# Pacing indirect stores, larger pieces for the down weights, and a later start of the loads of result rows, in a two-layer decoder kernel

## The reference, cut to what matters

```python
def moe_swiglu(hn, w_router, w_gate, w_up, w_down):      # 8 experts, top 2, hidden width 3584
    xt = hn.reshape(T, D)                                # T = 256, D = 1024
    top_logit, top_idx = lax.top_k((xt @ w_router).astype(jnp.float32), TOP_K)
    gates = jax.nn.softmax(top_logit, axis=-1)
    ...                                                  # rows sorted by expert, padded to blocks
    def expert_block(args):
        xb, e = args
        hid = jax.nn.silu(xb @ w_gate[e]) * (xb @ w_up[e])
        return hid @ w_down[e]
    ...                                                  # y[token] += gate * row, for both choices
```

## Time and profile before

| | us |
|---|---|
| median of 3 runs | 1377.39 (1375.36 to 1378.34) |
| the profiled execution, its own time | 1371.37 |
| its span, first to last instruction | 1369.5 |
| TensorE busy | 1314.4 (96%) |
| VectorE, ScalarE, GpSimd busy | 360.5, 243.4, 53.7 |

### The profile page before, as it was taken

How to read it: one execution, slowest core, us unless ns; L and a number is a source line. 1 busy time by engine, 2 the same in 40 slices (tenths; PEclk the granted TensorE clock), 3 DMA queues, 4 the chain that set the end, 5 groups by cost and what they waited for, 6 DMA issues and landing times.

```text
span 1369.5 us, 32426 instructions
## 1 busy us (share of the span) xinstructions
PE 1314.4 (96%) x14601; PEld 860.1 (63%) x14601; DVE 360.5 (26%) x505; ACT 243.4 (18%) x364; POOL 53.7 (4%) x47
## 2 busy tenths in 40 slices
PE   6998999999899689999999999999999999999998
PEld 6997899988777335855755764774572353354244
DVE  5875555554874501101101101100100110110111
ACT  5463544443642000000000000000000000000000
POOL 0001000000000130000000000000000000001500
PEclk9999999999999899999999999999999999999999
DMA  9972465564521789699999999999999999999996
GB/s 322 350 262 59 148 191 186 185 229 161 201 76 62 305 314 346 255 418 368 407 418 417 406 416 418 404 412 420 407 411 420 398 409 420 405 407 418 407 409 255
DMA packets 128647, 442.52 MB, mean 323 GB/s; under 512 B 9396, under 2 KB 55812, under 8 KB 112132
## 3 DMA queue, kind: packets, MB, share of 16 engines
q1 hardware_dynamic: 122352, 424.75, 80.2%
q10 hardware_dynamic: 4820, 11.53, 2.3%
q0 software_dynamic: 1344, 4.20, 0.8%
HBM read 434.12 MB, written 12.08 MB: 326 GB/s over the span
## 4 chain that ended last, share of the span: by engine, by line
PE 79%; DMA 9%; DVE 4%; ACT 3%; issue 3%; SPq 1%; ACTq 0%; POOL 0%; DVEq 0%; POOLq 0%
PE bank L1701 38%; PE bank L1713 16%; PE bank L1344 7%; PE bank L1345 6%; PE bank L1346 6%; DMA dn<-in_moe_w_down 4%; DMA raw<-in_moe_w_gate 3%; ACT w_hi L569 2%; DMA raw<-in_moe_w_up 2%; PE bank L1601 1%; PE bank L1549 1%; SPq L443 1%; DVE w_lo L836 1%; PE bank L1482 1%; PE bank L1691 0%
## 5 line engine op out<-in xcount | busy, mean ns | idle before, releaser
L1701 PE MATMUL bank<-raw,xT 128*32 128x512 f32 (+1 forms) x4608 | 452.9, 539 | 8.9 <-issue 4.6
L1701 PEld LDWEIGHTS bank<-raw,xT 128*32 128x32 f32 x4608 | 194.4, 110 | 255.5 <-issue 206.0
L1713 PE MATMUL bank<-dn,hidT 128*32 128x256 f32 x5376 | 294.5, 379 | 2.3 <-DMA dn<-in_moe_w_down 2.2
L1713 PEld LDWEIGHTS bank<-dn,hidT 128*32 128x32 f32 x5376 | 215.9, 110 | 80.0 <-DMA dn<-in_moe_w_down 7.6
L1315 DVE TENSOR_TENSOR e_hid<-e_silu,bank 128x512 f32<-128x512 f32 (+1 forms) x48 | 26.9, 616 | 556.6 <-PE bank L1701 556.6
L836 DVE TENSOR_TENSOR w_lo<-raw,w_hi 128x2048 fp32r<-128x2048 f32 x62 | 141.5, 2291 | 107.5 <-ACT w_hi L569 107.4
L1701 PE MATMUL bank<-up_more,xT 128*32 128x384 f32 (+1 forms) x1536 | 157.2, 539 | 1.0 <-DMA up_more<-in_moe_w_gate 1.0
L1344 PE MATMUL bank<-ht_hi,w_hi 128*128 128x256 f32 x480 | 134.2, 280 | 4.7 <-DVE w_lo L909 3.2
L1345 PE MATMUL bank<-ht_lo,w_hi 128*128 128x256 f32 x480 | 133.4, 278 | 0.0
L1346 PE MATMUL bank<-ht_hi,w_lo 128*128 128x256 f32 x480 | 133.4, 278 | 0.0
L569 ACT ACTIVATE w_hi<-raw 128x2048 fp32r<-128x2048 f32 x62 | 118.6, 1918 | 46.2 <-PE bank L1346 42.4
(11 more groups left out here) (262 smaller groups left out, 835.8 us busy)
## 6 DMA issues: line engine op xcount, KB each, us to landing
dn<-in_moe_w_down SPq DMA_DIRECT2D x112, 1024.0 KB, 15.0
raw<-in_moe_w_gate SPq DMA_DIRECT2D x48, 1024.0 KB, 20.5
raw<-in_moe_w_up SPq DMA_DIRECT2D x48, 1024.0 KB, 15.8
raw<-in_moe_w_gate SPq DMA_DIRECT2D x48, 768.0 KB, 12.5
raw<-in_moe_w_up SPq DMA_DIRECT2D x48, 768.0 KB, 10.5
up_more<-in_moe_w_gate SPq DMA_DIRECT2D x16, 1024.0 KB
up_more<-in_moe_w_up SPq DMA_DIRECT2D x16, 1024.0 KB
raw<-in_hgrn_w_in SPq DMA_DIRECT2D x15, 1024.0 KB, 12.8
```

Of the source, the lines that this page charges most:

```text
L1701: ins = nc.tensor.matmul(out_banks[j][GTOK * c:GTOK * c + GTOK, 0:w], xT[:, j, kt, :], chunk[:, c], start=kt == 0, stop=kt == KT - 1)
L1713: ins = nc.tensor.matmul(banks[6 + j // 2][GTOK * c:GTOK * c + GTOK, 256 * (j % 2):256 * (j % 2) + 256], hidT[sup][:, g, m, :], dn[:, i % ...
```

## The change

Three edits. (1) Each of GpSimd's 16 indirect stores of token rows is issued only after one more up chunk of item 0 has been used. (2) A down chunk puts rows 2p and 2p + 1 of its 256 into partition p, which are 8 KB in one piece. To have the hidden units in the matching order, the array's column group c takes hidden columns 64c to 64c+63 of every 256, and VectorE's transposes into `hidT` pick the even and the odd ones apart; they are now one for each of the three row groups, so `hidT_ready` counts 6 in an item instead of 2. (3) GpSimd's wait for the stored items is followed by a wait for the last item's last transposes, before the four indirect loads of result rows.

```diff
     def down_source(e, i):
         r = 256 * i
-        return a["moe_w_down"][0][bass.ds(e, 1), r:r + 256, :].rearrange("e (k p) c -> p (e k) c", p=P)
+        return a["moe_w_down"][0][bass.ds(e, 1), r:r + 256, :].rearrange("e (p k) c -> p (e k) c", k=2)
...
                     for c in range(4):
+                        pool.wait_ge(up_used, 8 * t + 4 * i + c + 1)
+                        pool.sem_inc(pool_pace, 1)
                         to = bass.IndirectOffsetOnAxis(ap=slot[:, t, i, c:c + 1], axis=0)
...
             pool.wait_ge(y_stored, n_before * 16)
+            pool.sem_inc(pool_pace, 1)
+            pool.wait_ge(hidT_ready, n_before * (2 * GRPS) + 2 * GRPS)
             pool.sem_inc(pool_pace, 1)
...
-                    nc.vector.transpose(hidT[sup][:, :, :, :].rearrange("p j m t -> p j (m t)"), e_hid[:, :, 0:w]).then_inc(hidT_ready, 1)
-                    dve.wait_ge(hidT_ready, n * 2 + (sup + 1))
+                    for j in range(GRPS):
+                        nc.vector.transpose(hidT[sup][:, j, :, :].rearrange("p (m k) t -> p m k t", k=2),
+                                            e_hid[:, j, 0:w].rearrange("p (m i k) -> p m k i", k=2, i=GTOK)).then_inc(hidT_ready, 1)
+                    dve.wait_ge(hidT_ready, n * (2 * GRPS) + (GRPS * sup + GRPS))
...
-                chunk = up_slot(i)[:, 0:4 * w].rearrange("p (m c i) -> p c m i", c=4, i=GTOK)
+                chunk = up_slot(i)[:, 0:4 * w].rearrange("p (m c i) -> p c m i", c=4, i=2 * GTOK)
...
                     if i == 0:
                         pe.wait_ge(yb_ready, n * 2 + 1)
-                        pe.wait_ge(hidT_ready, n * 2 + 1)
+                        pe.wait_ge(hidT_ready, n * (2 * GRPS) + GRPS)
                     if i == 8:
-                        pe.wait_ge(hidT_ready, n * 2 + 2)
+                        pe.wait_ge(hidT_ready, n * (2 * GRPS) + 2 * GRPS)
```

## The result

The changed kernel takes 1357.95 us (median of 4 runs, 1355.14 to 1359.29), the kernel before beside it 1377.87. The ratio is 0.9854, with a 95% interval of 0.9832 to 0.9877. Forecast were 1360.0 us, within 1354 to 1372.5. The profiled execution has a span of 1353.2 us, against 1369.5, and a time of 1357.36 us.

What follows compares the result with a forecast made beforehand. The prediction took TensorE's pace of 108.4 us an item as the floor, with DMA engines nearly as full. 11.0 + 6.4 + 0 = 17.4 us off 1371.37 gave 1354.0, plus 6.0 carried over: 1360.0 us, range 1354 to 1372.5.

Steps and rivals of the forecast that it cites:

- The paced stores, -11.0: Item 0's up products: spacing the 16 stores removes the slow stretch of TensorE, 11.0 us off.
- each store slows TensorE: Item 0's up products: a store slows TensorE by itself, so pacing only spreads the 11.0 us, gain 0.
- the pile does: Item 0's up products: the pile of unfinished stores slows TensorE, so pacing gains all 11.0 us.
- 8 KB pieces, -6.4: Down chunks' transfers: 0.061 us less for each of 105 chunks, 6.4 us off.
- The loads of result rows, 0: Last item: four stops of some 3.7 us go, but the same bytes delay down chunks instead; gain 0.
- The covers: Last down products: GpSimd's later chain stays hidden with 3.6 us of slack; the three transposes' extra time is hidden too, cost 0.
- B: Rival, item 0: the slow stretch stays, belonging to the first pass through the loop; only 6.4 comes, 1371.0 us; chance 0.17.
- C: Rival, down chunks: the size of a piece is worth nothing, 11.0 alone comes, 1366.4 us; chance 0.12.
- E: Rival: slow stretch stays and piece size is worth nothing, no change, 1377.4 us; chance 0.07.
- D: Rival, the tail: loads of result rows land late and the last additions wait, slower, 1387 us; chance 0.06.

Runs made afterwards that it cites:

- the serial one: Changed kernel with each of the 16 stores issued when the one before it has landed, without regard to TensorE: 1359.76 us.
- late burst: Changed kernel with all 16 stores in one burst after 9 up chunks of item 0: 1357.47 us, and 1368.47 us when run again in a later session.
- the kernel with early loads: Changed kernel with the loads of result rows begun when the last item but one is stored, as before: 1355.69 us.
- the 4 KB run: Changed kernel with down chunks in 4 KB pieces, the old order of hidden rows and the old transposes: 1365.13 us.
- the loads in two pairs: Changed kernel with the second pair of result-row loads issued after GpSimd's first addition: 1358.39 us.
- two bursts of 8: Changed kernel with the 16 stores in two bursts, at up chunks 1 and 9 of item 0: 1357.85 us, and 1364.98 us when run again.

## Why the prediction was right, point by point

The sum was 17.4 us off the profiled execution's span; the items' time is 17.6 shorter. The median moved by more, 19.9 us, and why isn't known. That it fell only 2.1 us from the forecast is in part luck: the prediction put the median 6.0 us above the profiled execution's time, and here it stands 0.6 above, while that execution itself took 1357.36 us instead of 1354.0.

- *The paced stores, -11.0.* Measured -11.1 by item 0's up products in the two profiles, -10.9 and -11.4 by undoing and doing the edit alone. The choice between "each store slows TensorE" and "the pile does" was made by the first stores of the burst running beside full pace, and its outcome held: paced, the stores cost nothing. That it is the pile of unfinished stores isn't shown. The only run that held the pile at one store, the serial one, fell in the session in which a burst did no harm; there the late burst's stores landed after 6.0 us (the median) and were issued every 1.27, so that by an estimate four or five were unfinished at once, and nothing slowed. Two of the readings were also coarser than told: the 102 matmuls "at full pace" took 12.26 us where 10.9 is full pace (0.1073 each), so that the slowing starts before the first gap; and "the DMA engines are not full" is true of 490 to 495 us only, for their share is 1.00 from 480 to 484 and 0.82 from 484 to 490. Full engines alone don't do it all the same, as TensorE keeps its pace beside them for all of items 1 to 3. That the 11 us would reach the end also held: in the changed kernel the DMA engines still run dry before the first down products (0 GB/s from 540 to 545 us). But the gain isn't to be had in every session: in one of five, going by the time of the kernel before, a burst cost nothing.
- *8 KB pieces, -6.4.* Measured -6.7 with the edit undone (by the medians of the same session 9.4, against the kernel with early loads, with more noise); the rates are 418 to 419 against 408 to 410 GB/s, as read from the old trace. It was the reading of two kinds of transfer in one trace, side by side, that gave the number before the change was run. The rule of the Trainium skill in DMA: Bandwidth & Descriptors, Specifications, that transfers are at line rate from 512 bytes on, doesn't agree with these rows: 4 KB pieces moved 2.4% slower than 8 KB pieces of the same tensor. The measurement decides, with the reserve that the rows' order changed along with the size; in a stream that is the bound for 800 us, 2.4% of a third of the bytes are some 6.4 us by an estimate, and 6.7 were measured.
- *The loads of result rows, 0.* Measured 0.3. The loss is 3.4 us (forecast 3.7), and it stands in the last down products. Its make-up was not as forecast: in the profile of the changed kernel 2.1 us of it are the slowing of TensorE beside the loads, and only the rest can be waits for weights. I take it that the one takes the place of the other, since TensorE and the weights run level and a slowed TensorE needs its weights later. No run tests this alone, but it fits that the session without slowing shows about the same loss with no gaps but waits for weights.
- *The covers.* GpSimd's chain ended 37.4 us after the down products began (forecast 36.3), 5.0 us ahead of VectorE's first addition. The three transposes took 1.50 us instead of 1.38 (forecast 1.74 to twice that); the stride cost nothing to speak of. TensorE's up products of one item stayed at 72.2 us with the new pattern of reading.
- *Rivals.* B fell by the late burst, C and E by the 4 KB run, D by the slack of 5.0 us: the second load landed 17.5 us after the first was issued (1309.19 to 1326.70), as it had before (17.25).

What stays open is by what means a burst of indirect stores slows TensorE, and why it didn't in one session. The runs show the place, the size and the growth of the effect, not the resource, and they don't part the number of unfinished stores from their rate. That the kernel before had no slow stretch in that session is argued from its time; there is no profile of it from there.

## What to carry to other kernels

Where the loss has the name "issue", lay the timelines of all engines beside the gaps: here the partner was an engine whose instructions seemed to cost nothing. Space out indirect DMAs by the progress of the engine that they disturb, and let the last of them end before the point at which another queue waits for them. Where a stream of weights is the bound, compare the rates of its kinds of transfer in the trace; bring the slower kind to the very shape that the faster one has, if the reordering can be paid in places that have cover. Larger was not better at every size here (6 KB was slower than 4 KB). Moving bytes about inside a saturated part of the kernel gained nothing. Whether letting part of them land after the last byte that is waited for gains anything isn't shown: the loads in two pairs gained 1.0 us of items' time and nothing that the medians show.

## What the hardware showed that I had not expected

A burst of 16 indirect stores of 128 x 1 KB, one every 1.27 us, slowed TensorE from some 9 us into it (first gap at 11) until 2.5 us after it, 11 to 12 us lost; two bursts of 8 lost 5.5 us together, the second more than the first; one store every 2.57 us lost nothing. Four indirect loads of 128 x 4 KB went with the same on a small scale beside down products (about 2 us) and not beside up products, where TensorE ran at full pace between the waits for weights (15.64 us for 144 matmuls in the run with early loads). During the slow stretches the weight loads of the array start in steps of 0.7 us or a multiple of it, as here in the kernel before (start, us, instructions, idle before):

```profile
486.51 0.14 PEld L1701 LDWEIGHTS bank<-raw,xT 128*32 128x32 f32 x2 [1.27 <-issue]
487.22 0.11 PEld L1701 LDWEIGHTS bank<-raw,xT 128*32 128x32 f32 x1 [0.56 <-issue]
487.93 0.11 PEld L1701 LDWEIGHTS bank<-raw,xT 128*32 128x32 f32 x1 [0.61 <-issue]
488.62 0.14 PEld L1701 LDWEIGHTS bank<-raw,xT 128*32 128x32 f32 x3 [0.59 <-issue]
```

One session of five showed none of this. And up chunks of 6 KB pieces moved no faster than down chunks of 4 KB pieces: 400 to 406 GB/s against 408 to 411, with 8 KB at 418 to 421; I have no explanation and no run that tells.
